# Four panels of the condition's product taken off TensorE and summed on VectorE

## What is computed

```python
cond = jax.nn.silu(c)
mod = (cond @ w_ada[l] + b_ada[l])[:, None, :]                  # [1, 6 * 1024]
sh1, sc1, gt1, sh2, sc2, gt2 = jnp.split(mod, 6, axis=-1)
h = rmsnorm(x, g_norm_mix[l]) * (1.0 + sc1) + sh1
c_q, c_kv, k_pe, dil, gates = jnp.split(h @ w_in[l], split_at, axis=-1)
o_a = mla_attention(...)                                        # 8 heads
# 3 groups of dilated attention, 8 heads: o_b
x = x + gt1 * ((g_a * o_a + g_b * o_b) @ w_out[l])
h2 = rmsnorm(x, g_norm_ffn[l]) * (1.0 + sc2) + sh2
x = x + gt2 * expert_choice_ffn(h2, ...)                        # 16 experts, 384 MB of weights
```

## Time and profile before

| | |
|---|---|
| median of three runs | 2500.11 us (2499.89 to 2506.11) |
| profiled execution, span | 2495.1 us; the page gives no time of its own for it outside the span |
| busy share of TensorE, VectorE, ScalarE | 88%, 37%, 14% |
| HBM read | 635.86 MB, 255 GB/s over the span |

### The profile page before, as it was taken

One profiled execution on the slowest core, in us unless ns is written; L12 is line 12 of the kernel. 1 busy time (PEld: TensorE's weight loads), 2 busy tenths in 40 slices (PEclk: granted clock), 3 DMA queues, 4 the chain that ended last, 5 costly groups with the idle time before them and its releaser, 6 DMA issues.

```text
span 2495.1 us, 28601 instructions
## 1 busy us (share of the span) xinstructions
PE 2199.1 (88%) x11574; PEld 1550.5 (62%) x11574; DVE 923.4 (37%) x2074; ACT 355.7 (14%) x715; POOL 1.0 (0%) x15
## 2 busy tenths in 40 slices
PE   7999999997677767666666899999999999999999
PEld 5878888862222222222222488788888888888888
DVE  6899885131110000000010085626232355523233
ACT  2231211120000000000000022411010115101011
POOL 0000000000000000000000000000000000000000
PEclk9999999998878787778788999999999999999999
DMA  7526574489999999999999973135444332453420
GB/s 283 189 77 227 197 242 135 169 362 428 427 428 428 428 429 428 429 428 429 428 428 427 423 272 121 56 110 194 165 139 166 136 123 85 169 202 136 167 101 17
DMA packets 148517, 638.15 MB, mean 256 GB/s; under 512 B 10293, under 2 KB 54846, under 8 KB 120526
## 3 DMA queue, kind: packets, MB, share of 16 engines
q1 hardware_dynamic: 147774, 635.71, 64.9%
q10 hardware_dynamic: 656, 1.22, 0.1%
HBM read 635.86 MB, written 1.05 MB: 255 GB/s over the span
## 4 chain that ended last, share of the span: by engine, by line
PE 69%; DMA 28%; DVE 1%; ACT 1%; issue 0%; SPq 0%; DVEq 0%; ACTq 0%
DMA arena<-in_w_down_dram 18%; PE PS L1802 17%; PE PS L1162 15%; PE PS L1815 8%; PE PS L1072 7%; DMA arena<-in_w_gate_dram 5%; DMA arena<-in_w_up_dram 4%; PE PS L1521 4%; PE PS L1393 2%; PE PS L1573 2%; PE PS L1633 2%; PE PS L1766 2%; PE PS L1513 1%; PE PS L1409 1%; PE PS L1591 1%; PE PS L1885 1%
## 5 line engine op out<-in xcount | busy, mean ns | idle before, releaser
L1521 PE MATMUL PS<-arena,hT 128*32 128x512 f32 x2048 | 316.8, 762 | 150.0 <-DMA arena<-in_w_up_dram 118.8
L1802 PE MATMUL PS<-arena 128*128 128x256 f32 x1920 | 416.7, 379 | 0.0
L1802 PEld LDWEIGHTS PS<-arena 128*128 128x128 f32 x1920 | 364.6, 190 | 49.8
L1521 PEld LDWEIGHTS PS<-arena,hT 128*32 128x32 f32 x2048 | 66.3, 128 | 376.5 <-DMA arena<-in_w_up_dram 192.3
L1162 PE MATMUL PS<-hT,arena 128*128 128x256 f32 (+1 forms) x1136 | 251.4, 381 | 0.7 <-ACT hT L731 0.7
L1573 PE MATMUL PS<-arena,hT 128*32 128x512 f32 x1008 | 172.5, 821 | 89.3 <-DMA arena<-in_w_down_dram 82.0
L1931 DVE SCALAR_TENSOR_TENSOR arena<-arena 128x512 f32<-128x512 f32 (+2 forms) x514 | 246.5, 548 | 0.8
L1162 PEld LDWEIGHTS PS<-hT,arena 128*128 128x128 f32 (+1 forms) x1136 | 211.4, 188 | 38.0 <-issue 8.0
L1928 DVE TENSOR_SCALAR arena<-arena,cols 128x256 f32<-128x256 f32 x162 | 66.3, 409 | 377.8 <-ACT arena L977 356.4
L1815 PE MATMUL PS<-arena 128*128 128x256 f32 x896 | 195.7, 379 | 0.0
L1934 DVE TENSOR_TENSOR hT<-hT,PS 128x512 f32<-128x512 f32 x16 | 16.4, 1027 | 474.6 <-PE PS L1521 474.6
(11 more groups left out here) (312 smaller groups left out, 1786.1 us busy)
## 6 DMA issues: line engine op xcount, KB each, us to landing
arena<-in_w_gate_dram SPq DMA_DIRECT2D x64, 2048.0 KB, 40.6
arena<-in_w_up_dram SPq DMA_DIRECT2D x64, 2048.0 KB, 40.7
arena<-in_w_down_dram SPq DMA_DIRECT2D x63, 2048.0 KB, 38.0
arena<-in_ffn_w_up_dram SPq DMA_DIRECT2D x32, 2048.0 KB, 8.5
arena<-in_w_in_dram SPq DMA_DIRECT2D x36, 1024.0 KB, 7.9
arena<-in_ffn_w_down_dram SPq DMA_DIRECT2D x16, 2048.0 KB, 7.8
arena<-in_w_ada_dram SPq DMA_DIRECT2D x12, 2048.0 KB, 11.6
arena<-in_ssd_w_in_dram SPq DMA_DIRECT2D x10, 2048.0 KB, 10.5
```

The costliest lines, as they stand in the source:

```text
L1521: mm = pe.matmul(PS[32 * f:32 * f + 32, 1 + half, :], xe[:, 32 * (2 * pi + k):32 * (2 * pi + k) + 32], w[:, k, 512 * f:512 * f + 512], sta ...
L1802: mm = pe.matmul(PS[:, n, T * half:T * half + T], slot(TAIL_SLOT[j], 8, 512)[:, k, P * n:P * n + P], hs[:, k, :], start=(k == 0), stop=(k ...
```

## The change

Panels 8 to 11 of `w_ada` are no longer multiplied on TensorE. They are loaded later, behind dil panels 11, 14, 15 and 16, in the same ring. VectorE multiplies each of a panel's two 128x2048 halves by its column of the condition and adds it to `ada_acc`, a buffer of 2048 columns over memory that the bias table used (one multiplication, then seven multiply-and-adds, each on 128x2048). TensorE then sums over the 128 partitions with four matmuls whose stationary operand is 32 columns of ones (`ada_summed`, behind step 32), and the row is copied out, transposed and biased as before, but in round 3. A slot that holds a summed panel is freed by VectorE (semaphore `sum_used`) in place of `used`.

```diff
+        if summed_after(j) is not None:
+            out.append("ada_sum")
 def ada_after(j):
-    if j < 4:
-        return 4 + j
-    return 3 + j if 5 <= j <= 8 else None
+    return 4 + j if j < 4 else None
+def summed_after(j):
+    return {11: 0, 14: 1, 15: 2, 16: 3}.get(j)
...
+        ada_acc = arena[:, MISC + 2976:MISC + 2976 + 2048]
...
+                if (name, j) in ST.behind_sum:
+                    sp.wait_ge(s["sum_used"], ST.behind_sum[name, j])
...
+            def load_sum(n):
+                taken, before = ST.sum_frees[n]
+                if taken:
+                    sp.wait_ge(used, taken)
+                if before is not None:
+                    sp.wait_ge(s["sum_used"], before)
+                si = ST.sum_slots[n]
+                sp.dma_start(slot(si, 2, 2048), w_ada[:, 2 * n:2 * n + 2, 4096:6144]).then_inc(slot_in[si], 16)
...
+                if summed_after(j) is not None:
+                    load_sum(summed_after(j))
...
             def ada_row(g):
-                act.wait_ge(used, ST.pos["ada"][4 * g + 3] + 1)
+                if g < 2:
+                    act.wait_ge(used, ST.pos["ada"][4 * g + 3] + 1)
+                else:
+                    act.wait_ge(s["sum_ps"], 1)
...
-                    if d == 35:
+                    if d == 66:
                         ada_row(2)
...
+            def ada_summed():
+                pe.wait_ge(s["mod_ready"], 3)
+                pe.wait_ge(s["sum_used"], 4)
+                for q in range(4):
+                    mm = pe.matmul(PS[32 * q:32 * q + 32, 7, :], ones[:, 0:32], ada_acc[:, 512 * q:512 * q + 512],
+                                   start=True, stop=True, skip_group_check=True)
+                mm.then_inc(s["sum_ps"], 1)
...
-                        if p // 2 == 9:
-                            ada_turn(2)
+                    if p == 32:
+                        ada_summed()
+                    if p == 33:
+                        ada_turn(2)
...
+            def ada_sum(n):
+                dve.wait_ge(slot_in[ST.sum_slots[n]], ST.sum_need[n])
+                w = slot(ST.sum_slots[n], 2, 2048)
+                for kk in range(2):
+                    k = 2 * n + kk
+                    if k == 0:
+                        ins = ts(ada_acc, w[:, kk, :], condT[:, k:k + 1], None, ALU.mult)
+                    else:
+                        ins = stt(ada_acc, w[:, kk, :], condT[:, k:k + 1], ada_acc, ALU.mult, ALU.add)
+                    if kk == 0:
+                        link("mix_tmp", ins)
+                ins.then_inc(s["sum_used"], 1)
+                dve.wait_ge(s["sum_used"], n + 1)
...
                 if q < 2:
                     bias_adds(6)
-                    modulation(q + 1)
-                mix(a0)
-                mix(a0 + 1)
-                if q < 2:
-                    bias_adds(6)
-                if q == 1:
-                    gain(A2, "g_norm_ffn", 32, 4)
-                    bias_fold(4)
+                if q == 0:
+                    modulation(1)
+                if q == 2:
+                    ada_sum(0)
+                    ada_sum(1)
+                if q == 3:
+                    modulation(2)
+                    gain(A2, "g_norm_ffn", 32, 4)
                     ...
+                mix(a0)
+                if q == 2:
+                    ada_sum(2)
+                mix(a0 + 1)
+                if q < 2:
+                    bias_adds(6)
+                if q == 1:
+                    bias_fold(4)
+                if q == 2:
+                    ada_sum(3)
```

More of the change, by code:

```diff
@@ L140, in put @@
             last[phys] = p
-        p = 0
-        for name in early_stream():
-            put(name, p % RING_A, p, 2 if name == "dil" else 1)
+        p, summed = 0, {}
+        self.sum_slots, self.sum_need, self.sum_frees, self.behind_sum = [], [], [], {}
+        for i, name in enumerate(early_stream()):
+            phys = i % RING_A
+            before = summed.pop(phys, None)
+            if name == "ada_sum":
+                loads[phys] += 1
+                self.sum_slots.append(phys)
+                self.sum_need.append(16 * loads[phys])
+                self.sum_frees.append((last[phys] + 1, before))
+                summed[phys], last[phys] = len(self.sum_slots), -1
+                continue
+            put(name, phys, p, 2 if name == "dil" else 1)
+            if before is not None:
+                self.behind_sum[name, len(self.pos[name]) - 1] = before
             p += 1
@@ L254 @@
         "rows_t", "cols_ready", "x_t", "x_ready", "cond_ready", "ada_row", "ada_col", "mod_ready",
-        "dve_chain", "rope_ready", "pos_done", "bias_hot", "bias_dve", "bias_fold", "near_ready", "far_t", "far_bt", "far_ps", "far_hot", "far_out", "far_ready", "sq_ready", "sq_added", "ss_ps",
+        "dve_chain", "rope_ready", "pos_done", "bias_hot", "bias_dve", "bias_fold", "far_t", "sum_used", "sum_ps", "far_ps", "far_hot", "far_out", "far_ready", "sq_ready", "sq_added", "ss_ps",
         "std_ready", "rstd_ready", "h_ready", "h1_act", "h1_dve", "pj_ps", "pj_ev", "rot_ps", "rope_tmp", "rope_out",
@@ L1121, in ada_rows @@
                 if jj == 0 and g:
-                    pe.wait_ge(s["mod_ready"], 2 if g == 1 else 3)
+                    pe.wait_ge(s["mod_ready"], 2)
                 w = slot(ST.slots["ada"][j], 2, 2048)
@@ L1175, in _ @@
                 if t == 1:
-                    pe.wait_ge(s["near_ready"], 1)
+                    pe.wait_ge(s["pos_done"], 2)
                     for c in range(TC):
@@ L1181, in _ @@
                 if t == 2:
-                    pe.wait_ge(s["far_bt"], 1)
+                    pe.wait_ge(s["pos_done"], 3)
                     pe.wait_ge(s["cols_ready"], 1)
@@ L2081, in _ @@
                                            AX.X, ALU.add))
-            dve.memset(tiny[:, 119:120], 0.0).then_inc(s["near_ready"], 1)
+            dve.memset(tiny[:, 119:120], 0.0).then_inc(s["pos_done"], 1)
             bias_hot(0)
             dve.wait_ge(s["far_t"], 1)
-            dve.tensor_copy(far_bucket, PS[0:16, 2, 0:T]).then_inc(s["far_bt"], 1)
+            dve.tensor_copy(far_bucket, PS[0:16, 2, 0:T]).then_inc(s["pos_done"], 1)
             for i in range(2):
```

## The result

| | before | after |
|---|---|---|
| median of 20 runs each | 2502.29 us (2496.18 to 2512.33) | 2496.41 us (2489.05 to 2504.47) |
| ratio, 95% interval | | 0.9971 [0.9962, 0.9981] |
| profiled execution, its time / its span | not given / 2495.1 us | 2496.19 / 2494.2 us |

The change makes the kernel faster: by the ratio 7.3 us, with ends of 4.8 and 9.5. The medians differ by 5.9 us and the means by 6.6, so no single figure here is sharper than a microsecond or two. The forecast was 7.1. The two profiled executions differ by only 0.9 us in span. So the comparison goes by stretches, not by totals.

A forecast was written before the change was run, and what follows sets the result against it. TensorE was taken to bound the changed stretch: 8.19 us removed less 1.12 added gives 7.1 us, VectorE's work hidden, so 2500.1 - 7.1 = 2493.0 us, range 2490.8 to 2499.0.

The forecast's parts named there:

- TensorE bounds the stretch, and a microsecond there is one of the path: From 289 to 489 us the chain runs on TensorE, so each microsecond taken off it shortens the path.
- Removed 8.19 us: Group 2's four panels on TensorE: 7.41 us, plus 0.78 for the slower steps behind them.
- `ada_summed` 0.93 + 0.19: TensorE's new four matmuls of ones: half a panel's 1.85 us, plus the slower step behind, 1.12 us.
- the rival without overlap: The four matmuls of ones run one behind the other: gain 4.5 us, 2495.6 us; chance 0.05.
- VectorE 18.2 us, hidden: Eight passes over 128x2048 behind round 2's `norm_part`, 1.8 + 7 x 2.35 us, fitting in VectorE's idle time.
- Deadlines: Moved loads and sums in rounds 1 to 3 arrive in time; smallest slack 5 us, at dil panel 16.
- The gain is carried through the experts: At the experts the long DMA stream's start follows TensorE, so the 7.1 us are kept to the end.
- The reload 7 us earlier and the second block moved by 7: Signs in the new profile: first reload of an expert slot and the second block both 7 us earlier.
- The rival that the gain stops at the experts: Loads ahead of the experts are the limit and hold the stream: result 2500.1 us; chance 0.05.
- The output projection at 481.7: Sign behind the last step: the output projection starts at 488.73 - 7.1 = 481.7 us.
- a start later than 483: Sign against the prediction: an output projection starting after 483 us makes it wrong.
- The time outside the span, 5.0 us: Median of the runs 5.0 us above the profiled span of 2495.1, taken as unchanged; gain subtracted from 2500.1.

The follow-up runs named there:

- the single small matmul: Kernel before, with one matmul of 32 columns for the eight of each group 2 panel, loads kept: 2489.0 us, one run, against 2499.93.

## Why the prediction was right, point by point

1. *TensorE bounds the stretch, and a microsecond there is one of the path.* Right, shown in both directions (6.9 us of matmuls added give 6.91 in the stretch, 6.7 taken away give 6.7, and 6.5 at the last gate).
2. *Removed 8.19 us.* Right: the undisturbed steps take 20.74, and the stretch is 7.00 shorter with 1.19 added. The part of 0.19 to 0.21 us for the step behind a panel is confirmed by the single small matmul, which leaves it in place.
3. *`ada_summed` 0.93 + 0.19.* Slightly too small: 0.99 to 1.00 + 0.19. I had halved the time of eight matmuls, and the 0.14 us that a batch costs once does not halve. The four overlap completely in a row of batches (0.86 each), so the rival without overlap falls. The Trainium skill (TensorE: Matmul & The Clock Gate, Measured speedup vs the span model) states 3.07 times for four row tiles; by that a batch would be an estimated 1.13 us. Measured: 0.99 to 1.00 for one batch alone, 3.5 times, and four times in a row of batches.
4. *VectorE 18.2 us, hidden.* Seven passes took 2.35 each, as said; the first 1.28 in place of 1.8, so 17.7 in all. That they are hidden is right, even at twice the length. (Section 2 of the page before has VectorE at 5 tenths in slice 7, not at 1 as I had written ahead of the prediction; nothing hung on it, since the stretch was read in finer windows.)
5. *Deadlines.* VectorE in round 1: no wait of TensorE. Smallest slack said 5 us, for dil panel 16: it was 7.4 (there at 441.1, step 32 at 448.5). S3's sum was 5.9 us ahead of the scores and 7.5 ahead of `ada_summed`, said 8 and 10. S3 took 13.3 us to land, I had reckoned with 11 to 12; all that was issued two microseconds late, with TensorE.
6. *The gain is carried through the experts.* Right for what arrives there: the reload is earlier by 4.6 us in the mean and the last gate by 3.5 us (1424.9 and 1421.4), with a scatter of up to 3.8 in the stretch between and perhaps 1 to 2 us lost in it. The reload 7 us earlier and the second block moved by 7, which I had named as signs, did not come in any profile of the changed kernel. The timed runs give 7.3 and 6.5. The rival that the gain stops at the experts falls, by the experiment that keeps the old loads above all.
7. *The output projection at 481.7.* It started at 483.6 to 483.9. I had named a start later than 483 as a sign that the prediction is wrong. By that sign this step failed: not the stretch (7.00 us shorter, said 7.07) but its start was off by 2.4 us in the mean, about 1.6 of it by the drop of the clock in front. I had taken for granted that nothing moves ahead of the edit.
8. *The time outside the span, 5.0 us.* Wrong: in the kernel before it is 1.7 to 1.9 in every run that has both numbers, in the changed one 1.8 to 3.0 (2.0 for the profiled one). The rest of the 5.0 was scatter: the profiled execution before was a fast one. It did no harm, since I subtracted the gain from the median. But the median shown, 2500.11, was itself low: over 20 runs it is 2502.29. So my 2493.0 came out 3.4 us below the measured 2496.41, 2.2 by this and 1.2 because the medians differ by 5.9.

So the mechanism and the size of the stretch are right and shown. That the ratio gives 7.3 us, so near to 7.1, is partly luck: in the profiles 2.4 us are lost in front, some more at the experts, and the timed runs of the kernel before hold about 5 us that its profiles do not have.

## What to carry to other kernels

Where one engine is full and another idles, a product with one row is cheap to move: multiply and add over the rows on VectorE, and let TensorE do only the last sum with ones. What decides is not VectorE's length, of which twice as much was hidden too, but which load stands behind which in the queue. List each moved load with the moment at which its data are due, and keep several microseconds there. Judge a gain of a few microseconds by the stretch in the chain that the edit touches, which repeats to 0.01 us, and then by many timed runs; two spans alone would have said 0.9. Look at what stands in front of the stretch too: a change can move with it something that no step of the sum holds.

## What the runs showed of the hardware

- A single drop of TensorE's granted clock to 1.2 GHz, behind waits of 1.8 to 2.3 us, cost about 1.6 us (a tile of eight matmuls 5.20 in place of 3.72). It appeared in all four executions of one program, in three of five variants of it, and in none of four executions of another that does the same work up to there; equal waits there left the clock at the upper level.
- Four matmuls of 512 columns in four quarters take 0.86 us in a row of batches, what 512 columns take in a row of full-width matmuls. One batch alone takes 1.00, and the full-width step behind it is 0.19 slower, however many batches there were.
- VectorE's multiply-and-add takes 2352 ns on 128x2048 float32, its multiplication by a column 1283 ns, little more than half.
- The same program's timed runs scatter with a standard deviation of 3.7 to 4.0 us over 20 runs. The stretch of the experts took 885.8 to 886.1 us in four executions before and 884.9 to 888.7 in four after, with the same loads in it; in a variant of the changed kernel it took 892.9.
